# The last feed-forward by one Strassen level: up and down products, with the gates kept in HBM

## The reference, cut to what matters

```python
mix = jnp.concatenate([attn.astype(h.dtype), rec], axis=-1) @ w_out[l]
h = h + rmsnorm_2(mix, g_post_mix[l])
u = rmsnorm_2(h, g_pre_ffn[l])
f = jnp.square(jax.nn.relu(u @ w_ff1[l])) @ w_ff2[l]
h = h + rmsnorm_2(f, g_post_ffn[l])
return h[:, N_META:]
```

## Time and profile before

| | |
|---|---|
| Median of 3 runs | 2532.38 us |
| Lowest and highest of them | 2531.85 and 2533.91 us |
| Span of the profiled execution | 2530.1 us |
| Own time of the profiled execution | not listed apart from the three runs |
| Mean granted clock of TensorE | 0.951 |
| TensorE, matmuls | 2382.2 us busy, 94% of the span, 11665 instructions |
| VectorE | 1332.1 us, 53%, 2131 instructions |
| ScalarE | 886.7 us, 35%, 1383 instructions |
| GpSimd | 576.6 us, 23%, 434 instructions |
| HBM read and written | 139.18 MB and 5.77 MB |

### The profile page before, as it was taken

How to read it: one execution, slowest core, us unless ns; L and a number is a source line. 1 busy time by engine, 2 the same in 40 slices (tenths; PEclk the granted TensorE clock), 3 DMA queues, 4 the chain that set the end, 5 groups by cost and what they waited for, 6 DMA issues and landing times. The chain is left out here.

```text
span 2530.1 us, 31119 instructions
## 1 busy us (share of the span) xinstructions
PE 2382.2 (94%) x11665; PEld 2015.4 (80%) x11665; DVE 1332.1 (53%) x2131; ACT 886.7 (35%) x1383; POOL 576.6 (23%) x434
## 2 busy tenths in 40 slices
PE   8989699989999999999999989689999999999996
PEld 5779588877888888888887989568788888888885
DVE  7699666665643443444445575663833333444435
ACT  5478555453421111111113571675411111111112
POOL 2021222215321222222121211114222222222213
PEclk9975699999999999999999999899999999999997
DMA  9025100023211111111110100013111111111101
GB/s 360 17 91 151 43 13 12 23 84 109 79 39 50 50 43 49 50 50 50 50 58 2 49 25 26 17 49 102 43 50 43 50 50 50 50 48 43 50 25 67
DMA packets 45668, 146.07 MB, mean 58 GB/s; under 512 B 5872, under 2 KB 10128, under 8 KB 45200
## 3 DMA queue, kind: packets, MB, share of 16 engines
q1 hardware_dynamic: 45584, 144.96, 17.3%
HBM read 139.18 MB, written 5.77 MB: 57 GB/s over the span
## 5 line engine op out<-in xcount | busy, mean ns | idle before, releaser
L158 PE MATMUL down<-g_hi,o_hi 128*128 128x512 f32 (+1 forms) x704 | 273.3, 388 | 2.3 <-DVE work L1860 1.3
L159 PE MATMUL down<-g_lo,o_hi 128*128 128x512 f32 (+1 forms) x704 | 272.4, 387 | 0.0
L160 PE MATMUL down<-g_hi,o_lo 128*128 128x512 f32 (+1 forms) x704 | 272.4, 387 | 0.0
L1847 DVE TENSOR_TENSOR relu<-relu 128x1024 f32<-128x1024 f32 x32 | 39.6, 1237 | 330.9 <-ACT relu L1710 330.9
L158 PE MATMUL up<-m_hi,i_hi 128*128 128x512 f32 x480 | 187.3, 390 | 1.3 <-DVE m_lo L1835 1.3
L160 PE MATMUL up<-m_hi,i_lo 128*128 128x512 f32 x480 | 186.8, 389 | 0.0
L159 PE MATMUL up<-m_lo,i_hi 128*128 128x512 f32 x480 | 186.8, 389 | 0.0
L1862 DVE TENSOR_TENSOR work<-down,work 128x512 f32<-128x512 f32 x224 | 147.5, 684 | 56.8 <-PE down L160 56.8
L158 PEld LDWEIGHTS down<-g_hi,o_hi 128*128 128x128 f32 x704 | 134.0, 190 | 29.5 <-DVE work L1860 1.7
L159 PEld LDWEIGHTS down<-g_lo,o_hi 128*128 128x128 f32 x704 | 133.9, 190 | 26.5
L2833 DVE SCALAR_TENSOR_TENSOR x<-down,mod,x 128x512 f32<-128x512 f32 x160 | 120.0, 750 | 66.4 <-PE down L160 64.5
(11 more groups left out here) (494 smaller groups left out, 5821.9 us busy)
## 6 DMA issues: line engine op xcount, KB each, us to landing
ada<-in_ada_w SPq DMA_DIRECT2D x32, 512.0 KB, 3.6
i_raw<-in_w_ff SPq DMA_DIRECT2D x32, 512.0 KB, 3.5
o_raw<-in_w_ff SPq DMA_DIRECT2D x32, 512.0 KB, 3.5
work<-in_f_w_u SPq DMA_DIRECT2D x22, 512.0 KB, 3.5
work<-in_f_w_v SPq DMA_DIRECT2D x22, 512.0 KB, 3.6
work<-in_f_w_out SPq DMA_DIRECT2D x22, 512.0 KB, 4.4
work<-in_ada_rows SPq DMA_DIRECT2D x16, 512.0 KB, 8.5
wo_raw<-in_a_w_o SPq DMA_DIRECT2D x16, 512.0 KB, 3.5
```

What stands on the lines that cost most here:

```text
L158: nc.tensor.matmul(out, w_hi, x_hi, start=start, stop=False)
L159: nc.tensor.matmul(out, w_hi, x_lo, start=False, stop=False)
L160: return nc.tensor.matmul(out, w_lo, x_hi, start=False, stop=stop)
L1847: nc.vector.tensor_tensor(r[:, :], r[:, :], r[:, :], ALU.mult).then_inc(square_s, 1)
```

## The change

A pair x of up tiles (256 features, 1024 inputs) times u (1024 inputs, two halves of tokens) is taken as a product of 2 x 2 blocks, and done with seven block products in place of eight (Strassen's scheme in Winograd's form). Both sides need sums of blocks. The same is done for a down pair (1024 outputs in two halves, 2 x 128 features, two token halves).

- A **unit** is one block product: 12 matmuls. There are 16 x 7 = 112 up units and 15 x 7 = 105 down units; the last pair's down products stay as they were, in three pieces. `Units` writes the order out: first P1 and P2 of the pairs 0 to 3 (these need only the first token half), then the other five of each of them, then all seven of each pair from 4 on. All down units come after all up units, in three groups of five pairs; within a group all P1, then all P2, and so on.
- **Weights.** The high part is made per unit (128 x 512) by ScalarE two units ahead (`weights_high(n + 2)`). P1, P2 and P4 take raw blocks, whose low part is made by GpSimd; the other four take sums of blocks, which VectorE makes three units ahead (`weights_sum`), with the low part also on VectorE (`weights_low`). The parts lie in a ring of three.
- **The side of u.** Seven operands of 4 k-tiles (`b_hi`, `b_lo`): u11, u21, u22 and four sums, made once between the residual and the first units. The squares of h are summed in between.
- **Up results.** Each unit has a PSUM bank. VectorE adds them up to the four blocks of a pair (`out11`, `out_u2`, `out22`, `out12`, `out21`); relu and square are on ScalarE for two blocks and on VectorE for two; VectorE makes the four sums of gates that the down half needs (`blk(x, 4)` to `blk(x, 7)`, in `out12`, `sums32`, `sum4`). The eight blocks of a pair (2 MB) are written to HBM, from one of two buffers that lie where `xs` was. For that, `xs` is itself written to HBM first (`x_keep`, 4 MB) and read back in the down half.
- **Down half.** A unit reads one gate block (256 KB) back from HBM (`load_gate`, four buffers, in the order of the units) and splits it on ScalarE and VectorE (`gate_high`, `gate_low`). Five pairs of a kind add up in the four PSUM banks of a set; then the set is copied (first group, ScalarE) or added (`add_sum`, VectorE, 128 x 2048) to `total`. In the last group VectorE joins the totals to the four quarters of the result (`join`, 128 x 2048).
- `o_raw`, `o_hi` and `o_lo` of the stage before stay in use for the mixer's output only; all tiles of the stage are placed by hand at offsets that share memory.

The diff, cut to what the text speaks of:

```diff
+EARLY, GROUP = 4, 5
+class Units:
+    def __init__(self, n_up, n_down):
+        self.n_up = n_up
+        self.up = [(x, i) for x in range(min(EARLY, n_up)) for i in (P1, P2)]
+        self.up += [(x, i) for x in range(n_up) for i in range(7) if x >= EARLY or i > P2]
+        self.down, first = [], 0
+        self.groups = []
+        while first < n_down:
+            self.groups.append(range(first, min(first + GROUP, n_down)))
+            self.down += [(n_up + p, i) for i in range(7) for p in self.groups[-1]]
+            first += GROUP
...
+                def load_gate(b):
+                    w, i = units.all[UP + b]
+                    if b >= 4:
+                        sp.wait_ge(gate_lo_s, b - 3)
+                    at_block = BLOCK[i] * 512
+                    sp.dma_start(gate_raw[b % 4][:, :], d["gates"][w - PAIRS][:, at_block:at_block + 512])\
+                        .then_inc(g_loaded[b % 4], 16)
...
+                for x in range(PAIRS):
+                    if x == LAST:
+                        sp.wait_ge(done, units.at[(x, P1)] + 1)
+                        for j in (2, 3):
+                            load_down(j, 0)
+                            load_down(j, 1)
+                        sp.wait_ge(done, units.at[(x, P2)] + 1)
+                        load_down(4, 0)
+                        load_down(4, 1)
+                        for b in range(4):
+                            load_gate(b)
+                    sp.wait_ge(dve_lo, units.low[units.at[(x, P3)]])
+                    if x + 2 < PAIRS:
+                        load_up(x + 2, 0)
+                    else:
+                        load_down(x + 2 - PAIRS, 0)
+                    sp.wait_ge(pool_lo, units.low[units.at[(x, P4)]])
+                    if x + 2 < PAIRS:
+                        load_up(x + 2, 1)
+                    else:
+                        load_down(x + 2 - PAIRS, 1)
+                    sp.wait_ge(t_s, 4 * x + 4)
+                    sp.dma_start(d["gates"][x], gates[x % 2]).then_inc(spilled[x % 2], 16)
+                sp.wait_ge(done, UP)
+                sp.dma_start(end_o_raw[:, 0, :], d["w_ff2"][2 * LAST]).then_inc(end_o_loaded, 16)
+                sp.dma_start(end_o_raw[:, 1, :], d["w_ff2"][2 * LAST + 1]).then_inc(end_o_loaded, 16)
...
+                for b in range(4, len(units.down)):
+                    load_gate(b)
+                    if b == 12:
+                        for i in range(2):
+                            sp.wait_ge(spilled[i], 16 * (PAIRS // 2))
+                        sp.wait_ge(kept, 16 * KT)
+                        for k in range(KT):
+                            sp.dma_start(xs[:, k, META:META + T], d["x_keep"][k]).then_inc(back, 16)
+                    w, i = units.down[b - 4]
+                    p = w - PAIRS
+                    if p + GROUP < LAST and i == P3:
+                        sp.wait_ge(dve_lo, units.low[UP + b - 4])
+                        load_down(p + GROUP, 0)
+                    if p + GROUP < LAST and i == P4:
+                        sp.wait_ge(pool_lo, units.low[UP + b - 4])
+                        load_down(p + GROUP, 1)
...
+                def up_unit(n):
+                    x, i = units.all[n]
+                    hi, lo = w_parts(n)
+                    bank_free(x, i)
+                    weights_ready(n)
+                    for kk in range(HALF):
+                        if x == 0:
+                            pe.wait_ge(t_lo_s, HALF * (P7, P6, P5, P3, P4).index(i) + kk + 1)
+                        mm = three_products(nc, UP_BANK[i], hi[:, col4[kk]], lo[:, col4[kk]], b_hi[i][:, kk, :],
+                                            b_lo[i][:, kk, :], kk == 0, kk == HALF - 1)
                     mm.then_inc(done, 1)
...
+                def down_unit(n):
+                    w, i = units.all[n]
+                    b, s = n - UP, step_of(n)
+                    j, g = (w - PAIRS) % GROUP, (n - UP) % 3
+                    hi, lo = w_parts(n)
+                    if j == 0:
+                        set_free(s)
+                    weights_ready(n)
+                    pe.wait_ge(gate_lo_s, b + 1)
+                    for t in range(HALF):
+                        mm = three_products(nc, sets[s % 2][:, t, :], hi[:, col4[t]], lo[:, col4[t]], gate_hi[g][:, :],
+                                            gate_lo[g][:, :], j == 0, j == GROUP - 1)
+                    mm.then_inc(done, 1)
...
+                def weights_high(n):
+                    w, i = units.all[n]
+                    if n >= 5:
+                        act.wait_ge(done, n - 2)
+                    elif n > 2:
+                        act.wait_ge(wo_done, N)
...
+                def out11(x):
+                    gate_buffer(x)
+                    if x < EARLY:
+                        dve.wait_ge(p_s, 2 * EARLY)
+                        nc.vector.tensor_tensor(blk(x, 0), early_p[x][0], early_p[x][1], ALU.add).then_inc(c11_s, 1)
+                    else:
+                        dve.wait_ge(done, units.at[(x, P2)] + 1)
+                        dve.wait_ge(p_s, EARLY + x + 1)
+                        nc.vector.tensor_tensor(blk(x, 0), B_BANK, own_p1[x % 2], ALU.add).then_inc(c11_s, 1)
...
+                def out12(x):
+                    dve.wait_ge(done, units.at[(x, P3)] + 1)
+                    nc.vector.tensor_tensor(blk(x, 1), D_BANK, y, ALU.add).then_inc(c12_s, 1)
+                    dve.wait_ge(c12_s, x + 1)
+                    relu_squared(x, 1)
+                    dve.wait_ge(g_s, 2 * x + 1)
+                    dve.wait_ge(act_g, 2 * x + 1)
+                    nc.vector.tensor_tensor(blk(x, 4), blk(x, 1), blk(x, 0), ALU.subtract).then_inc(t_s, 1)
...
+                def sums32(x):
+                    dve.wait_ge(act_g, 2 * x + 2)
+                    nc.vector.tensor_tensor(blk(x, 6), blk(x, 3), blk(x, 1), ALU.subtract).then_inc(t_s, 1)
+                    dve.wait_ge(t_s, 4 * x + 2)
+                    nc.vector.tensor_tensor(blk(x, 5), blk(x, 6), blk(x, 0), ALU.add).then_inc(t_s, 1)
...
+                def gate_low(b):
+                    dve.wait_ge(gate_hi_s, b + 1)
+                    nc.vector.tensor_tensor(gate_lo[b % 3][:, :], gate_raw[b % 4][:, :], f32(gate_hi[b % 3][:, :]),
+                                            ALU.subtract).then_inc(gate_lo_s, 1)
...
+                def add_sum(i, q, to):
+                    s = 7 * q + i
+                    dve.wait_ge(done, load_step(q, i, GROUP - 1) + 1)
+                    if q == 1:
+                        dve.wait_ge(act_sum, i + 1)
+                    nc.vector.tensor_tensor(to, sets[s % 2][:, :, :], total[i][:, :, :], ALU.add).then_inc(dve_sum, 1)
...
+                for kk in range(HALF):
+                    t3_full(kk)
+                    t2_full(kk)
+                weights_sum(8)
+                for kk in range(HALF):
+                    part_low(P7, 0, kk)
+                for kk in range(HALF):
+                    t4_full(kk)
+                weights_low(8)
+                weights_sum(9)
+                for kk in range(HALF):
+                    part_low(P6, 4, kk)
+                weights_low(9)
+                weights_sum(10)
+                for kk in range(HALF):
+                    difference(kk)
+                for kk in range(HALF):
+                    t1_low(kk)
+                weights_low(10)
+                weights_sum(11)
+                dve.wait_ge(h_total, 1)
+                for kk in range(HALF):
+                    b22_low(kk)
+                for kk in range(HALF):
+                    part_low(P4, 8, kk)
                 for k in range(1, KT):
                     add_h(1, k)
+                for n in range(9, ALL):
+                    if n - 1 < UP:
+                        unit_out(*units.all[n - 1])
+                    w, i = units.all[n]
+                    if n == UP:
+                        sums32(LAST)
+                        sum4(LAST)
+                    if n + 2 < ALL:
+                        if not units.on_pool(n + 2):
+                            weights_low(n + 2)
+                        if n + 2 >= UP:
+                            gate_low(n + 2 - UP)
+                    if n + 3 < ALL and not units.on_pool(n + 3):
+                        weights_sum(n + 3)
+                    if n >= UP:
+                        q, j = (w - PAIRS) // GROUP, (w - PAIRS) % GROUP
+                        if j == 0 and 7 < step_of(n) <= 7 * (GROUPS - 1):
+                            s = step_of(n) - 1
+                            add_sum(s % 7, s // 7, total[s % 7][:, :, :])
+                        elif q == GROUPS - 1:
+                            last_group(i, j)
```

879 lines of the change are left out of this document (605 added, 274 removed).

## The result

The changed kernel takes **2503.59 us** (median of 4 runs, 2501.51 to 2504.08), the kernel before, run beside it on the same chip, 2533.14 us (4 runs, 2531.85 to 2534.61). The ratio is 0.9885 with a 95% interval of 0.9873 to 0.9896: 29.6 us less by the medians, where 42 were forecast. The time lies inside the range of 2462 to 2522. The profiled execution is the fastest of the four, 2501.51 us with a span of 2499.5; the span was forecast at 2487.6.

The account below looks back on a forecast made before the run. The prediction took TensorE's matmuls to bound the feed-forward; 2432.4 us without stalls plus 55.2 of stalls gave a span of 2487.6, a median of 2490, with an 8-in-10 range of 2462 to 2522 us.

Parts of the forecast that it names:

- fewer matmuls and their price: Feed-forward on TensorE: 372 matmuls fewer at 0.2268 us each, 84.4 us less.
- the straight sum: Whole span without stalls: up start, 217 units, small blocks and the end from `last_down` make 2432.4 us.
- the first transition: From mixer to feed-forward: VectorE's chain delays units 8 to 11; 26.3 us of stalls.
- pairs 1 to 3: Early up pairs with five units left: VectorE's work exceeds their 13.6 us; 3.5 us lost in all.
- the bound of 17.7: Steady up pairs: VectorE's 13.9 us plus at most 3.8 of GpSimd locks fit into 19.05 us; no stall.
- up to down: Start of the down half: gates behind spills and weights on SP's queue; 14.9 us plus 4 of half clock.
- U: The time at which the down half would begin without stalls; gate 0 was forecast there at U + 5.4.
- the 6 us of the last group: End of the down half: joins and GpSimd operations overload VectorE in the P3 and P4 steps; 6 us of stalls.
- the lock between VectorE and GpSimd: Feed-forward: a VectorE operation with two SBUF inputs and a GpSimd operation exclude each other; VectorE may lose GpSimd's full length.
- Mostly hidden: Rival on the stalls: locks and dependent waits cost less than charged; 2445 to 2466 us, chance 0.1.
- VectorE paces the up pairs: Rival: VectorE sets the pace of up pairs, 20.5 us each, and of middle down steps; 2520 to 2530 us, chance 0.13.
- Slower than before: Rival: queueing and locks push up pairs above 22.6 us, costing the whole gain; 2549 us at 24, chance 0.05.

Follow-up runs that it names:

- e3_squares_pe: Changed kernel with the second token half's squares summed by 32 one-column matmuls on TensorE instead of VectorE's seven add_h, ScalarE's squares made earlier: 2495.41 us.
- e5_gates_rows: Changed kernel with first down gates and needed weight rows queued ahead of the spills, other weight rows later: 2481.61 us, ratio 0.9803.
- e2_sum_first: Changed kernel with VectorE making the weight sum of unit n + 3 before the low parts of unit n + 2 in the down half: 2490.3 us.
- e7_more_vector: Changed kernel with three extra unused 128 x 512 VectorE subtractions in each of up pairs 5 to 14: 2500.08 us, ratio 0.9877.
- e6_end_on_vector: Changed kernel with the last pair's four 1024-wide low-part subtractions moved from GpSimd to VectorE: 2498.53 us, ratio 0.9867.
- e8_all: Changed kernel with gates and rows reordered, weight sum first, squares on TensorE, and the last pair's low parts on VectorE: 2468.26 us, ratio 0.9751.
- e4_pool_zero: Changed kernel with GpSimd writing zeros instead of subtracting low parts in the last group and for the last pair: 2489.73 us, ratio 0.9839.
- e9_three: Changed kernel with gates and rows reordered, weight sum first, and squares on TensorE: 2466.38 us, ratio 0.9742.
- e10_all_p4: Changed kernel with gates reordered, weight sum first, squares on TensorE, last pair's and last group's P4 low parts on VectorE: 2463.97 us, ratio 0.9731.

## Why the prediction was right or wrong

**Right: fewer matmuls and their price.** 372 fewer, the first unit starts at 1784.82 (1785.0 set), and from 1851.52 to 2117.67 us 1175 matmuls start 0.2267 us apart, 2.72 per unit. The stalls of the table are counted from the straight sum's own positions, so that they add up to the span is no proof beyond this. The terms named as removed, 84.4 + 8.6 = 93.0 us, are less than the 97.7 between 2530.1 and 2432.4: the prediction did not name the 6.4 us by which the 2976 matmuls of the old loop take longer than 0.2268 us each, and it set the small blocks at 1 us in one sum and at 2.6 in the other.

**Right: the first transition.** Units 8, 10 and 11 start at 1817.62, 1827.50 and 1840.62; the sum of VectorE's work gave 1818.1, 1828.2 and 1840.7. The residual took 13.9 us (1791.55 to 1805.42) where 11.1 + 3 were set; `add_h` took 6.3 where 5.5 stood, which the 0.5 us by which unit 8 came early mostly hides. The 1.3 us for the squares was counted twice, once in the sum to unit 11 and once beside it. `e3_squares_pe` shows that this chain is the bound for unit 11: shorter by 6.3 us, it lets unit 11 start 6.3 us earlier, although unit 8 came 3.1 us later. That all three starts were met within 0.5 us is in part luck: the start, the residual and `add_h` were each off by 0.2 to 0.8 us, in both directions.

**Too dear: pairs 1 to 3.** 3.5 us were charged, none came. The charge was 13.9 + 1.0 = 14.9 us of VectorE's work in the 13.6 of such a pair. The row of the kernel after for these three pairs (stretch, its length, VectorE busy, clock, DMA share, GB/s) shows 38.89 us, 13.0 a pair:

```profile
1846.50:1887.30 40.80, 38.89 (x60) 1.00 0.48 181
```

That is 95% of the time, and TensorE came to them late and at half clock for seven matmul starts. Where it comes earlier, in `e3_squares_pe`, waits of 0.42 to 0.47 us do appear there, so the limit is near. In the steady pairs nothing was charged, rightly; the bound of 17.7 took each GpSimd operation as lost for VectorE in full, and it is busy 14.6 us. How much of the 14.6 is lock no run here tells.

**Right in mechanism, small by 3 us: up to down.** The waits at UP and UP + 4 and their releaser (a DMA behind one queue) came as written. The one between them was set at 1.2 us for unit 1's weights and 1.4 for VectorE at unit 2; it came as 3.35 us at unit 2 alone, for VectorE. Gate 0 is taken at 2123.95, 6.0 us behind U = 2117.9 (5.4 forecast), unit UP + 4 19.6 us late (14.9 and one half-clock stretch of 2 forecast). There are three stretches at half clock, not two: behind 2125.44, 2136.93 and 2148.37. `e5_gates_rows` shows the cause: with nothing but the order of the queue changed, 18.6 of the 22.0 us are gone, and the wait for VectorE is what is left.

**Wrong: "In a step of five units VectorE has at most 5 x 3 x 0.61 + 2.2 = 11.4 of 13.6 us: no stall", and with it the 6 us of the last group.** The sum of work was right (0.60 an operation, 2.28 for `add_sum`), but work is not the pace. The weight sum, ScalarE's cast and the low part are a ring with one unit of lead, and in the written order it turns in 2.64 us, not in 1.8. So a step of five units with its `add_sum` takes 14.56 us of 13.61, where the forecast counted 11.4. The lead of the first groups is used up by 2299 us, and from then on each set sum costs up to 0.95 us; VectorE comes late into the last group, where the joins and GpSimd are. Measured 18.4 us: 11.4 of waits, 3.4 of half clock behind the last group's, and some 3.6 in which matmuls start a little further apart, half of it right behind the waits. `e2_sum_first` shows it: with the order alone changed the small waits go, and some 8 us with them (9.8 less 1.5 of clock that is not its doing).

**Half right: the lock between VectorE and GpSimd.** The Trainium skill ("SBUF — State Buffer", "SBUF: two separate sides") has the two share a pair of ports, which whoever starts first holds for a whole instruction while the other is blocked. The forecast took from row and page only a cost for VectorE. The trace shows the other side, and over more than one instruction: 11.40 us for two GpSimd operations of 1.3, beside VectorE operations without a gap. The forecast left that side out. Of the 3.02 us wait for `w_lo` it is a part: the `g_lo` ahead of it took 1.2 us more than its 2.64, and the rest is that this `g_lo` stands ahead of the `w_lo` in GpSimd's order.

**The rivals.** "Mostly hidden" is excluded by 67 us of stalls. "VectorE paces the up pairs" is excluded by `e7_more_vector`; its second half, the down steps, was partly true, though by an order of work and not by its amount. In the pairs 1 to 3 VectorE sets the pace only once the chain before unit 11 is shortened (`e3_squares_pe`). Slower than before did not come near.

## What to carry to other kernels

Where two engines hand work to each other once per step, the sum of an engine's work says nothing about how fast it can catch up: lay out one period with the hand-overs, and start the part that the other engine needs first. At a change of phase list what stands in the DMA queue in bytes ahead of the first load that the next phase wants, and move that load, not the traffic: that was 18.6 us here at no cost. Work moved from GpSimd to VectorE helps only if what is left on GpSimd is not shut out by it. Small work put into an engine's gap is to be timed first: 32 one-column matmuls took 10.95 us, more than the 7.6 us gap that they were meant for.

## What was not expected of the hardware

- **VectorE can shut GpSimd out for about 10 us.** Two 128 x 512 subtractions on GpSimd took 11.40 us in `e6_end_on_vector` and 11.27 us in `e8_all`, beside VectorE operations with two SBUF operands, 0.68 to 2.28 us long and without gaps; undisturbed one takes 1.27 to 1.30 us. Beside GpSimd's fills in `e4_pool_zero` no row of VectorE grew.
- **The half clock came behind waits of 3 us too.** Behind the waits of 3.35 us (2136.93) and 3.02 us (2434.24) matmuls start 0.427 us apart for a while, which is the 1.2 GHz level. The forecast had taken it only from the wait of 4.7 us and the block of small matmuls of the kernel before. In `e9_three` it came behind waits of 2.33 and 2.69 us as well, and not behind one of 2.43 us before unit 11.
- **The DMAs' rate held with writes among the reads.** Between 2110 and 2122 us, with the spill, weights and gates in the queue, they moved 379 GB/s at full share, near the 405 of the weight loads; the 2 MB spills landed in 7.3 us (median).
- **The last 1.5 us.** In `e10_all_p4` TensorE stands 1.53 us ahead of `last_down`, and its row names no releaser. `last_down` waits for the last pair's low parts, which are VectorE's there: the last of them, a `g_lo` of 1.22 us, starts at 2405.75 and so ends at 2406.97, and `last_down` starts at 2407.06. In `e8_all` the two times are 2410.42 and 2410.52. So the work moved off GpSimd is late by that much.
